# Block 2's first two attentions: scores from queries stacked over 128 rows

## The reference

```python
s_c = jnp.einsum('bghqd,bgkd->bghqk', qq, kc) * scale       # first attention, compressed
s_s = jnp.einsum('bghqd,bgqkd->bghqk', qq, k_sel) * scale   # selected
s_w = jnp.einsum('bghqd,bgkd->bghqk', qq, kwb) * scale      # window
return gg[..., 0:1] * o_c + gg[..., 1:2] * o_s + gg[..., 2:3] * o_w
...
logits = jnp.einsum('bnqghd,bnkgd->bghnqk', q, kk) * scale  # second attention
```

## Time and profile before

| What | Value |
| --- | --- |
| Median of 3 runs | 2464.51 us (2463.87 to 2465.90) |
| Profiled execution | 2469.78 us, its span 2468.0 us, mean granted clock 0.983 |
| PE matmul busy | 2355.4 us (95%), 17448 matmuls |
| PE weight load busy | 2118.3 us (86%) |
| DVE, ACT busy | 1493.8 us (61%), 1229.5 us (50%) |
| DMA | 352.46 MB, mean 143 GB/s |
| First layer, `project_and_compress` | about 1242 to 1294 us |
| First layer, near attention's stage | about 1294 to 1396 us |
| First layer, second attention's steps | about 1396 to 1437 us |
| Second layer, the same | 1952 to 2003, 2003 to 2106, 2106 to 2147 us |

### The profile page before, as it was taken

The page is one execution under the profiler, slowest core; times in us unless marked ns, Lnnn a source line. Parts: engine busy times, 40 slices in busy tenths (PEclk is TensorE's granted clock), DMA queues, the critical chain, the costliest instruction groups (busy, mean ns, idle before and its releaser), DMA issues. The chain is left out here.

```text
span 2468.0 us, 45344 instructions
## 1 busy us (share of the span) xinstructions
PE 2355.4 (95%) x17448; PEld 2118.3 (86%) x17448; DVE 1493.8 (61%) x2689; ACT 1229.5 (50%) x1960; POOL 213.0 (9%) x240
## 2 busy tenths in 40 slices
PE   6998999999989999999999999999999989999998
PEld 3776577788778699999988899999999978998998
DVE  5468875453466865655476665654655666566654
ACT  6265744642347656434365554543543565555443
POOL 1012000000012000022000000221121000000320
PEclk8999999999999999999999999999999999999999
DMA  7311023444133044555552334455455442343552
GB/s 280 117 69 61 1 100 139 171 158 149 69 128 113 7 154 172 182 193 187 188 184 91 120 130 172 159 185 189 153 183 189 153 171 91 136 155 137 197 195 85
DMA packets 59444, 352.46 MB, mean 143 GB/s; under 512 B 6128, under 2 KB 17568, under 8 KB 18208
## 3 DMA queue, kind: packets, MB, share of 16 engines
q1 hardware_dynamic: 59152, 350.39, 39.6%
q10 hardware_dynamic: 144, 0.01, 0.0%
HBM read 346.15 MB, written 1.08 MB: 141 GB/s over the span
## 5 line engine op out<-in xcount | busy, mean ns | idle before, releaser
L239 DVE TENSOR_TENSOR w_lo<-ring,w_hi 128x1024 fp32r<-128x1024 f32 x638 | 811.3, 1305 | 491.9 <-ACT w_hi L225 491.3
L281 PE MATMUL psum<-x_hi,w_hi 128*128 128x256 f32 (+1 forms) x3376 | 1036.5, 307 | 25.9 <-DVE w_lo L239 13.4
L283 PE MATMUL psum<-x_hi,w_lo 128*128 128x256 f32 (+1 forms) x3376 | 1014.9, 301 | 0.0
L282 PE MATMUL psum<-x_lo,w_hi 128*128 128x256 f32 (+1 forms) x3376 | 1014.0, 300 | 0.0
L225 ACT ACTIVATE w_hi<-ring 128x1024 fp32r<-128x1024 f32 (+1 forms) x638 | 643.4, 1049 | 329.3 <-PE psum L283 158.1
L281 PEld LDWEIGHTS psum<-x_hi,w_hi 128*128 128x128 f32 x3376 | 641.5, 190 | 64.2 <-issue 16.1
L282 PEld LDWEIGHTS psum<-x_lo,w_hi 128*128 128x128 f32 x3376 | 641.8, 190 | 26.2 <-issue 1.7
L283 PEld LDWEIGHTS psum<-x_hi,w_lo 128*128 128x128 f32 x3376 | 641.5, 190 | 24.0
L1842 PE MATMUL psum<-h_lo,w_hi 128*128 (+1 forms) x640 | 179.8, 281 | 0.0
L1843 PE MATMUL psum<-h_hi,w_lo 128*128 (+1 forms) x640 | 179.8, 281 | 0.0
L1840 PE MATMUL psum<-h_hi,w_hi 128*128 (+1 forms) x640 | 179.8, 281 | 0.0
(11 more groups left out here) (319 smaller groups left out, 2880.0 us busy)
## 6 DMA issues: line engine op xcount, KB each, us to landing
ring<-wstream SPq DMA_DIRECT2D x320, 1024.0 KB, 4.8
x<-xT SPq DMA_DIRECT2D x2, 1024.0 KB, 8.1
x<-ctxT SPq DMA_DIRECT2D x2, 1024.0 KB, 10.7
rel_bias<-bias_by_distance SPq DMA_DIRECT2D x2, 1024.0 KB, 7.5
cst<-consts SPq DMA_DIRECT2D x1, 1534.0 KB, 10.7
wk<-wk_once SPq DMA_DIRECT2D x8, 128.0 KB, 4.1
kk_sw<-kk_sw SPq DMA_DIRECT2D x8, 128.0 KB, 5.9
out<-x SPq DMA_DIRECT2D x8, 128.0 KB, 2.0
```

Source lines behind the costliest of these rows:

```text
L239: dve.tensor_tensor(w_lo[:, c % 2, h], ring[:, (c + 2 * i) % RING, h], w_hi[:, c % 2, h].bitcast(F32), ALU.subtract).then_inc(split_done.s ...
L281: pe.matmul(o, w_hi[:, c, w_cols], hi, start=first, stop=False)
L282: pe.matmul(o, w_hi[:, c, w_cols], lo, start=False, stop=False)
L283: return pe.matmul(o, w_lo[:, c, w_cols], hi, start=False, stop=last)
```

## The change

The queries of the first and the second attention get a new kind of take, "st" for stacked. ACT and DVE now write, in place of a hi and a lo tile for the pair, one tile for each head: tile 0 has head 2p's hi part in rows 0 to 63 and its lo part in rows 64 to 127; tile 1 has head 2p+1's lo part in rows 0 to 63 and its hi part in rows 64 to 127. The keys, which lie twice over the rows already, are unchanged. A matmul of a stacked tile over 128 rows with the hi keys gives hi by hi plus lo by hi, and one with the lo keys the other two products (lo by lo is included now). So a step has four matmuls on 128 rows in the place of six on 64. The take of these four chunks of a layer is two ACT and two DVE instructions on 64 rows in the place of one each on 128. The third attention keeps its form, and so do both attentions of the first block.

The 32 steps of a layer that are changed are 8 with 16 keys, 12 with 128 and 12 with 256. Where they stand does not change.

```diff
@@ -757,6 +757,13 @@
                     if t >= self.SETS:
                         pe.wait_ge(biased.sem, self.base[biased] + 2 * (t - self.SETS + 1))
                     q, k = u["q"], u["k"]
+                    if "stacked" in u:
+                        for half in range(2):
+                            for e in range(2):
+                                mm = pe.matmul(self.score(t, half, k[e].shape[1]), q[half], k[e], start=e == 0,
+                                               stop=e == 1)
+                        mm.then_inc(scored.sem, 1)
+                        return
                     products = ((0, 0), (1, 0), (0, 1)) if len(q) == 2 else ((0, 0),)
                     for e, (qn, kn) in enumerate(products):
                         for half in range(2):
...
+        def stack_upper(act, o, a, scale):
+
+            low, high = slice(0, DH), slice(DH, P)
+            act.activation(o[0][low], a[low], ACT.Copy, scale=scale)
+            return act.activation(o[1][high], a[high], ACT.Copy, scale=scale)
+
+        def stack_lower(dve, o, a, scale):
+
+            low, high = slice(0, DH), slice(DH, P)
+            dve.scalar_tensor_tensor(out=o[0][high], in0=a[low], scalar=scale, in1=o[0][low].bitcast(F32),
+                                     op0=ALU.mult, op1=ALU.subtract)
+            return dve.scalar_tensor_tensor(out=o[1][low], in0=a[high], scalar=scale, in1=o[1][high].bitcast(F32),
+                                            op0=ALU.mult, op1=ALU.subtract)
...
+                        elif kind == "st":
+                            stack_upper(act, o, result(j), scale).then_inc(upper.sem, 1)
...
+                        if kind == "st":
+                            dve.wait_ge(upper.sem, u0 + halves.index(j) + 1)
+                            stack_lower(dve, o, result(j), scale).then_inc(acc_free.sem, 1)
...
@@ -2503,9 +2529,8 @@
                         if j in halves:
                             _, o, scale = plan[j]
                             dve.wait_ge(upper.sem, u0 + halves.index(j) + 1)
-                            if plan[j][0] == "kk":
-                                dve.scalar_tensor_tensor(out=o[1], in0=result(j), scalar=scale, in1=o[0].bitcast(F32),
-                                                         op0=ALU.mult, op1=ALU.subtract).then_inc(acc_free.sem, 1)
+                            if plan[j][0] == "st":
+                                stack_lower(dve, o, result(j), scale).then_inc(acc_free.sem, 1)
...
-                    common = dict(q=[a[:, pair, qt * P:qt * P + P] for a in qs], at=qt * P, pair=pair)
+                    common = dict(q=[a[:, pair, qt * P:qt * P + P] for a in qs], at=qt * P, pair=pair, stacked=True)
...
+                        u["stacked"] = True
```

More of the change, by code:

```diff
@@ L1935, in mix_stage, with queries @@
                 v_b = sb("v_b", [P, 2, 160], stack=st, side="right")
-                def queries(qs):
-                    return [("kk", tuple(t[:, m:m + 2, :] for t in qs), DH ** -0.5) for m in (0, 2)]
+                def queries(qs, kind):
+                    return [(kind, tuple(t[:, m:m + 2, :] for t in qs), DH ** -0.5) for m in (0, 2)]
                 def in_place_of(qs):
@@ L1952, in mix_stage @@
                         project_and_compress(layer, [("kv", kv_cmp, 1.0), ("kd", tuple(a[:] for a in kk_sw), 1.0),
-                                                     *queries(qa), ("r", v_sw[:], 1.0), ("r", v_b[:], 1.0)],
+                                                     *queries(qa, "st"), ("r", v_sw[:], 1.0), ("r", v_b[:], 1.0)],
                                              layer_norm(layer, 1), kkc, vc, v_b, gates, st3)
@@ L1962, in mix_stage @@
                     attend_and_project(near, forget, [
-                        *queries(qb), ("kd", (kkb[0][:], kkb[1][:]), 1.0), *queries(qc),
+                        *queries(qb, "st"), ("kd", (kkb[0][:], kkb[1][:]), 1.0), *queries(qc, "kk"),
                         ("kk", (kkf[0][:, 0:2, :], kkf[1][:, 0:2, :]), 1.0),
@@ L2076, in attend_and_project @@
             u0, c0, d0 = upper.n, copied.n, doubled.n
-            halves = [j for j, (kind, _, _) in enumerate(plan) if kind in ("kk", "kd")]
+            halves = [j for j, (kind, _, _) in enumerate(plan) if kind in ("kk", "kd", "st")]
             KEYS = 2
@@ L2144, in take @@
                         kind, o, scale = plan[j]
-                        if kind == "kk":
+                        if kind == "st":
+                            dve.wait_ge(upper.sem, u0 + halves.index(j) + 1)
+                            stack_lower(dve, o, result(j), scale).then_inc(acc_free.sem, 1)
+                        elif kind == "kk":
                             dve.wait_ge(upper.sem, u0 + halves.index(j) + 1)
@@ L2362, in project_and_compress @@
             c0, d0, s0 = copied.n, doubled.n, stored.n
-            halves = [j for j, (kind, _, _) in enumerate(plan) if kind in ("kd", "kk")]
+            halves = [j for j, (kind, _, _) in enumerate(plan) if kind in ("kd", "kk", "st")]
             def result(j):
@@ L2441, in _ @@
                             act.activation(o, a[:, :, 0:o.shape[2]], ACT.Copy).then_inc(acc_free.sem, 1)
-                        elif kind == "kk":
-                            act.activation(o[0], a, ACT.Copy, scale=scale).then_inc(upper.sem, 1)
+                        elif kind == "st":
+                            stack_upper(act, o, a, scale).then_inc(upper.sem, 1)
                         else:
```

## The result

The changed kernel takes 2472.67 us (median of 8 runs, 2466.74 to 2479.33) against 2463.69 us for the kernel before on the same chip (8 runs, 2458.18 to 2465.90). The ratio is 1.0038 [1.0025, 1.0051], so it is slower by about 9 us. The forecast was 2463.3 us, 1.2 us faster, and the time lies above its range.

A forecast was written before the change was run, and what follows sets the result against it. PE, busy 2355 of 2468 us, was taken as the bound. Per layer 1.7 + 0.95 - 2.0 - 1.45 = -0.8 us, two layers -1.6, clock +0.2 a layer: -1.2 us from 2464.5 gives 2463.3 us, range 2458 to 2469.

The forecast's parts named there:

- the edges: PE's score steps: long gaps on both sides of the 64-row matmuls go; L283 to L282 0.71 us (256 keys), 0.68 (128).
- pairs lost: Rival, each of the 64 steps: no edge saved, one slot of 0.12 us added; 2476 us with the takes; chance 0.07.
- the remaining gains: Cheaper score steps in the near stage behind L2613, -2.0 us a layer, and in the second attention, -1.45 us.
- the stalls in the projection: PE waits for DVE's delayed L239 ahead of the fifth and sixth chunk: 1.7 us a layer in all.
- a sign against it: Projection stage: the prediction is wrong if this stage comes out longer by more than 2.5 us.
- the first take of qb: Near stage, L820 behind the take: 0.5 us of PE's gain go, leaving PE at -0.3 us.
- the near stage up to L2613: Both takes of qb delay the ACT and DVE chain that PE waits for: +0.95 us a layer at L2613.
- +0.2 us a layer: Clock term: PE's idle stretch ahead of L2613 grows by 1.2 us, so half clock there may repeat or hit less work.
- more half clock: Rival: DVE's stalls in projection and ahead of L2613 add 1.5 us stretches in four places: +4.4 us, 2469 us; chance 0.13.
- Takes free: Rival: the split takes cost nothing on ACT and DVE, or slack suffices: -8.4 us, 2456.1 us; chance 0.06.
- Stalls smaller: Rival: stalls from the takes are half of 3.4 us a layer: -5 us, 2459.5 us; chance 0.14.

The follow-up runs named there:

- the repetition: The changed kernel built and measured once more, unaltered, with a second profile: 2474.68 us, ratio 1.0043 to the kernel before.
- `flatten` later: The changed kernel with DVE making the next weights' lo part (L239) ahead of `flatten` in the projection stage: 2469.94 us, 1.0019 to before.
- the fills: The changed kernel plus matmuls on constants into a free PSUM bank at four PE waits (8, 8, 8 and 10 a layer): 2468.31 us, 1.0011 to before.
- takes only: The kernel before with its layout and six matmuls kept, each of a layer's four takes split in two 64-row instructions: 2479.63 us, 1.0054 to before.
- steps on PE only: The changed kernel with single takes on 128 rows, four matmuls a step, no stacked layout (scores not the reference's): 2465.22 us, 1.0000 to before.

## Why the prediction was wrong

**Right: the edges.** L283 to L282 was to be 0.71 us (256 keys) and 0.68 us (128). It is 0.70 to 0.72 us with 256 and 0.68 us with 128, where 0.98 and 0.91 us stood. The rule of the Trainium skill that speaks against the change (TensorE: Matmul & The Clock Gate, Part 3, Packing small matmuls) would have made four slots dearer than three. The trace agrees with its small distance (the two of a pair start 0.004 to 0.016 us apart before) and not with the outcome: 0.98 us with three pairs and 0.71 us with four matmuls. Each group of pairs stands between matmuls on 128 rows and pays two edges. The rival "pairs lost" fell with it.

**Right: the remaining gains.** Rest of the near stage -1.73 and -1.74 us in the two layers (forecast -2.0); second attention -1.67 and -1.68 us (forecast -1.45).

**Right: the stalls in the projection.** They came at both places named, 1.06 and 0.58 us by the waits (forecast 1.7 us in all). The stage grew by 1.7 and 2.0 us. In the repetition it grew by 3.0 and 2.1 us, and the 3.0 lies beyond the 2.5 us that the prediction had named as a sign against it. The two pieces with the stalls were the same (24.27 and 6.46 us, after 24.27 and 6.47); the rest of the stage was longer, 22.51 instead of 21.18 us. It differs in the kernel before too (21.68 and 22.11 us), so it does not speak against the stalls. The 1.7 us of the first pair is in part luck. PE kept full clock behind both stalls, as the changed kernel's windows show. `flatten` later, which takes both away, gave the two pieces back.

```profile
1267.00:1273.00 6.00, 5.69 (x48) 5.72 (x48) 5.80 (x13) 2.49 (x3) 0.00 (x0) 1.00 0.59 189
1273.00:1280.00 7.00, 6.42 (x57) 6.25 (x56) 5.35 (x8) 4.17 (x9) 0.00 (x0) 1.00 0.55 169
```

**Near in its net, wrong in what it meant: the first take of qb.** The forecast had PE at -0.3 us behind it; it stands at -0.4 in the first pair's first layer and at +0.1 to +0.3 in the other three. Ahead of the wait PE had won 0.7 to 1.4 us (forecast 0.7), and that and DVE's own delay became idle time: the gap between the two matmul starts around the wait grew from 0.93 to 2.11 us. The forecast booked the lost gain as 0.5 us of time. It did not ask what an idle stretch more than twice as long brings.

**The step that failed: the near stage up to L2613, +0.95 us, and with it the clock at "+0.2 us a layer".** Measured +3.3 and +4.2 us. The forecast looked for the clock only at the stretch ahead of L2613, which was at half clock already. The half clock came some 12 us earlier, right behind the first take's wait, in 6 us full of matmuls. The piece from there to L2613 was to grow by 1.25 us; it grew by 3.7 and 4.1 us, and with the fills, at full clock, by 1.7 us. So 2.0 us in the first layer and 2.4 us in the second are the clock, and what is left, 0.4 us, is the take that was sized a little short (a pair took 1.42 us where the single take took 0.61, +0.8 for a forecast of +0.65). In the repetition the half clock behind the wait was shorter, PE waited 2.42 instead of 1.75 us for the next L827, and the piece was as long (14.1 us). With this step mended, the sum of the pieces is -1.6 + 2.3 + 3.25 = +4.0 us, and the traces have 382.6 - 378.3 = +4.3 us (the second layer's projection took 0.3 us more).

**From +4.3 to 9 us.** In the repetition the mixing is longer by 384.0 - 377.6 = 6.4 us. By the traces' clock records half clock takes 20.5 us of the two layers' mixing in both executions of before and 37.5 us in both of the change; 17 us more of it cost at most 8.5 us. Over all runs of a kernel the loss rises from 37 to 44 us, while the time without it hardly moves (2429.1 and 2428.5, 2431.5 in the repetition). That the clock is the cause of most of what the forecast missed is shown by the fills, which put work only where PE waited: half clock falls to 13.7 us, the mixing to 376.7 us, 1.4 us shorter than before, the mean clock goes from 0.9821 to 0.9856 and the excess over before from 9 to 3 us. That the 1.4 us is near the forecast's 1.6 is luck in part, since the fills also end the half clock behind L2613 that the kernel before has.

Some 3 to 5 us of the 9 are not in the mixing and stay open. The rest of the program is the same code, and in the two profiled pairs it was faster with the change, by 5.3 and 3.1 us. There two chances meet. The profiled executions of before had more half clock outside the mixing (65 and 61 us, with the change 52 and 54), and between 1434 and 1954 us of the first trace of the change 1348 projection matmuls followed at the shorter of the two distances named below, in before 35. That stretch took 514.5 us against 520.3, in the second pair 517.8 against 520.2. Most experiments have such a remainder: takes only is 9.3 us longer in the mixing and 13.5 by the medians, steps on PE only 5.1 us shorter and 1.0. It stays open too why the steps alone bring half clock around the last chunk and the kernel before doesn't.

**The rival that came nearest**, "more half clock" (0.13, 2469 us), had the mechanism. It was sized at one stretch of 1.5 us in each of four places, two of them in the projection, where none came; the stretch that did come stands behind the first take of qb, which it had not named. That its +4.4 us is near the +4.3 of the traces is luck. What spoke for it and was not weighed: the change lengthens DVE's work ahead of a wait of PE (0.66 to 1.26 us by the takes alone), and shortens PE's (to 1.84 us with both). "Takes free" fell: the pairs cost full price, and taking them out of the way (steps on PE only, rest -7 us) shows what that was. "Stalls smaller" fell with the stalls.

## What to carry to other kernels

Work added to an engine on which the one that sets the end waits, and work taken from the latter ahead of that wait, both turn into idle time. Its price is not only the time of the wait: look at the granted clock in the stretch behind each wait that grows. A gain that is spread over a program is to be priced together with the instructions that its layout needs on the other engines; here eight takes in halves ate the gain of sixty-four cheaper steps. Where idle stretches can't be removed, matmuls on constants kept the clock here, 34 a layer in four places together; in one place alone they brought no time.

## What the runs showed of the hardware

- An instruction on 64 rows cost as much as one on 128 (DVE's single take 0.68 us, ACT's 0.59 us): DVE's takes stand 0.69 us apart, though each writes to the other half of the rows than it reads. ACT's two at the first take of qb, in the changed kernel:

```profile
1308.62 0.58 ACT L2069 ACTIVATE x_hi<-psum 64x512 fp32r<-64x512 f32 x1
1309.20 0.59 ACT L2070 ACTIVATE x_lo<-psum 64x512 fp32r<-64x512 f32 x1
```

- The same projection matmuls run at one of two distances at full clock, and change between them without an idle stretch. Both are in the timeline of the changed kernel: 18 matmuls in 2.04 us ahead of the score step (0.113 us each), and 9 in 1.06 us from 1407.59 to 1408.65 behind it (0.118 us each). Which holds over long stretches differs between executions of one kernel (514.5 and 517.8 us for 1434 to 1954 in two of the change). One profiled pair can hide a difference of 9 us in this way.
- PE's stalls of 1.06 and 0.58 us in the projection were followed by full clock, the wait of 1.84 us in the near stage by half, and so was the one of 1.26 us there with the takes only. The length of a wait alone does not decide: the wait of 1.82 us ahead of the last projection chunk was followed by full clock in the changed kernel and by half clock with the steps on PE only (second line):

```profile
1387.56 0.39 PE L2024 MATMUL psum<-w_hi,x_hi 128*128 128x256 f32 x1 [1.82 <-DVE x_lo L2173]
...
1379.39 0.39 PE L2024 MATMUL psum<-w_hi,x_hi 128*128 128x256 f32 x1 [1.82 <-DVE x_lo L2168]
```
